# Inverting the delta rule's triangular blocks: 32-row blocks solved on VectorE, one level of TensorE products fewer

## What is computed

```python
m = jnp.einsum('bhncd,bhnsd->bhncs', k_beta, k) * decay
m = jnp.where(tri_strict, m, 0.0) + jnp.eye(CHUNK, dtype=jnp.float32)
rhs = jnp.concatenate([v * beta[..., None], k_beta * jnp.exp(g)[..., None]], axis=-1)
sol = lax.linalg.triangular_solve(m, rhs, left_side=True, lower=True, unit_diagonal=True)
u, w = sol[..., :dv], sol[..., dv:]
```

## Time and profile before

| | |
|---|---|
| median of 3 runs | 2465.13 us (2462.39 to 2465.59) |
| profiled execution, its own time | 2461.05 us |
| its span | 2459.3 us |
| TensorE matmul, busy | 2289.7 us, 93% |
| VectorE, busy | 1374.0 us, 56% |
| ScalarE, busy | 918.7 us, 37% |
| granted TensorE clock, mean | 0.972 |
| DMA | 328.93 MB, mean 134 GB/s |

### The profile page before, as it was taken

The page is one execution under the profiler, slowest core; times in us unless marked ns, Lnnn a source line. Parts: engine busy times, 40 slices in busy tenths (PEclk is TensorE's granted clock), DMA queues, the critical chain, the costliest instruction groups (busy, mean ns, idle before and its releaser), DMA issues. The chain is left out here.

```text
span 2459.3 us, 38535 instructions
## 1 busy us (share of the span) xinstructions
PE 2289.7 (93%) x13868; PEld 1852.7 (75%) x13868; DVE 1374.0 (56%) x2331; ACT 918.7 (37%) x1689; POOL 143.1 (6%) x183
## 2 busy tenths in 40 slices
PE   5789999999999999999999979899999999999887
PEld 3167787777778787878788758787887878787886
DVE  0334655546464646565654555656566565656665
ACT  3432424242433424242522363443424243342533
POOL 0000000000001000000100300000000000000002
PEclk8989999999999999999999989999999999999998
DMA  8974534243343435343545534433424343343554
GB/s 314 352 222 120 159 90 137 83 127 116 110 137 111 141 90 162 90 136 91 183 122 153 171 92 119 118 106 95 137 73 126 86 119 107 94 122 89 162 164 127
DMA packets 488882, 328.93 MB, mean 134 GB/s; under 512 B 48754, under 2 KB 452374, under 8 KB 488294
## 3 DMA queue, kind: packets, MB, share of 16 engines
q1 hardware_dynamic: 393750, 219.64, 31.6%
q10 hardware_dynamic: 94992, 108.09, 13.5%
q0 software_dynamic: 64, 0.20, 0.0%
HBM read 304.73 MB, written 23.13 MB: 133 GB/s over the span
## 5 line engine op out<-in xcount | busy, mean ns | idle before, releaser
L1808 PE MATMUL ps<-h_hi,w_hi 128*128 128x512 f32 (+1 forms) x2080 | 825.3, 397 | 18.1 <-DVE w_lo L1113 10.8
L1810 PE MATMUL ps<-h_hi,w_lo 128*128 128x512 f32 (+1 forms) x2080 | 768.1, 369 | 0.0
L1809 PE MATMUL ps<-h_lo,w_hi 128*128 128x512 f32 (+1 forms) x2080 | 767.6, 369 | 0.0
L1113 DVE TENSOR_TENSOR w_lo<-w_raw,w_hi 128x1024 fp32r<-128x1024 f32 (+1 forms) x300 | 365.4, 1218 | 290.6 <-ACT w_hi L660 251.4
L1808 PEld LDWEIGHTS ps<-h_hi,w_hi 128*128 128x128 f32 x2080 | 400.2, 192 | 125.3 <-issue 51.4
L660 ACT CAST w_hi<-w_raw 128x1024 fp32r<-128x1024 f32 (+1 forms) x300 | 311.5, 1038 | 369.5 <-PE ps L1810 188.0
L1810 PEld LDWEIGHTS ps<-h_hi,w_lo 128*128 128x128 f32 x2080 | 397.5, 191 | 68.5
L1809 PEld LDWEIGHTS ps<-h_lo,w_hi 128*128 128x128 f32 x2080 | 400.3, 192 | 49.8
L2089 PE MATMUL ps<-h_hi,w_hi 128*128 128x512 f32 (+1 forms) x448 | 157.8, 352 | 7.7 <-DVE h_lo L1113 6.6
L1648 POOL TENSOR_SCALAR small<-small 128x4 f32<-128x4 f32 (+3 forms) x51 | 20.5, 402 | 2254.5 <-DVE small L1488 987.4
L2090 PE MATMUL ps<-h_lo,w_hi 128*128 128x512 f32 (+1 forms) x448 | 151.7, 339 | 0.0
(11 more groups left out here) (199 smaller groups left out, 2769.7 us busy)
## 6 DMA issues: line engine op xcount, KB each, us to landing
w_raw<-in_w_in SPq DMA_DIRECT2D x260, 512.0 KB, 4.0
ada_raw<-in_w_ada ACTq DMA_DIRECT2D x128, 512.0 KB, 4.7
w_raw<-in_w_out SPq DMA_DIRECT2D x36, 448.0 KB, 3.8
arena<-in_w_ada SPq DMA_DIRECT2D x27, 512.0 KB, 8.4
arena<-in_w_out SPq DMA_DIRECT2D x28, 448.0 KB, 4.4
w_raw<-in_w_ada SPq DMA_DIRECT2D x19, 512.0 KB, 8.4
ada_raw<-in_w_ada SPq DMA_DIRECT2D x18, 512.0 KB, 8.3
arena<-decay_rows ACTq DMA_DIRECT2D x16, 512.0 KB, 6.2
```

The costliest lines, as they stand in the source:

```text
L1113: return V.tensor_tensor(o, a, b, op)
L1808: mm(o, w_hi[:, s, k], h_hi[:, kt, t0:], start=kt == 0, stop=False)
L1809: before_last = mm(o, w_hi[:, s, k], h_lo[:, kt, t0:], start=False, stop=False)
L1810: last = mm(o, w_lo[:, s, k], h_hi[:, kt, t0:], start=False, stop=kt == KT - 1)
```

## The change

The blocks that VectorE solves are 32 wide, so the product level from 16 to 32 goes. A block lies on four partitions: partition 32 q + b works on block b, on every fourth row of it (rows 4 i + q), so 8 rows each. All four hold the whole block of m (the read L590 becomes a broadcast to 128 partitions, 4 KB each). Row s of the inverse is found column by column: in step k the columns right of k get column k times row k of m taken off. Step k has k // 4 + 1 rows and 31 - k columns, a product and a subtraction. There are 31 steps in ten items (PIECES). The block stores and loads on SyncE are 4 DMAs in place of 8 each, and the solved blocks are stored by 4 DMAs in place of one. In the one full level left, inv is only formed in the quadrant that the corner step reads, so four of the eight matmuls and one of two merges shrink to 64x64. The slot tables are new.

```diff
-LEVELS = (16, 32, 64)
+LEVELS = (32, 64)
 BLK = LEVELS[0]
 NB = P // BLK
+SHARE = 4
+ROWS = BLK // SHARE
...
+        c[:, C_SHARE + q] = i // 32 == q
...
-        blocks = prod[0:2 * NT * NB].rearrange("p x c d -> p (x c d)")
-        blk_m, blk_s = [blocks[:, n * BLK * BLK:(n + 1) * BLK * BLK] for n in range(2)]
-        blk_t = blocks[:, 2 * BLK * BLK:4 * BLK * BLK]
+        blk_m = prod.rearrange("p x c d -> p (x c d)")
+        blk_s, blk_t = [inv_m[:, 0].rearrange("p c d -> p (c d)")[:, n * ROWS * BLK:(n + 1) * ROWS * BLK] for n in range(2)]
...
+        s_rows = blk_s.rearrange("p (i n) -> p i n", n=BLK)
+        s_diagonal = bass.AP(tensor=blk_s.tensor, offset=blk_s.offset,
+                             ap=[list(blk_s.ap[0]), [SHARE + BLK, ROWS], [1, SHARE]])
+
+        def eliminate(eng, own, steps):
+
             for k in steps:
-                up = SUB - 1 - k
-                term = t[:, :, 0:up, up:]
-                own.done(eng.tensor_tensor(term, m[:, :, 0:up, up:up + 1].to_broadcast(term.shape),
-                                           s_[:, :, up:up + 1, up:].to_broadcast(term.shape), ALU.mult))
-                own.done(eng.tensor_tensor(s_[:, :, 0:up, up:], s_[:, :, 0:up, up:], term, ALU.subtract))
-
-        def corner_product(eng, own, out_, a, b):
-
-            terms = blk_t.rearrange("p (r n k) -> p r n k", r=SUB, n=SUB)
-            own.done(eng.tensor_tensor(terms, a.unsqueeze(2).to_broadcast(terms.shape),
-                                       b.rearrange("p k n -> p n k").unsqueeze(1).to_broadcast(terms.shape), ALU.mult))
-            own.done(eng.tensor_reduce(out_, terms, AX, ALU.add))
-
-        def join_halves(eng, own):
-
-            spare = corner(blk_m, 1, 0)
-            corner_product(eng, own, spare, corner(blk_m, 0, 1), corner(blk_s, 1, 1))
-            corner_product(eng, own, corner(blk_m, 0, 1), corner(blk_s, 0, 0), spare)
-            own.done(eng.tensor_scalar(corner(blk_s, 0, 1), corner(blk_m, 0, 1), -1.0, None, ALU.mult))
+                rows = k // SHARE + 1
+                rest = BLK - 1 - k
+                term = blk_t[:, 0:rows * rest].rearrange("p (i n) -> p i n", n=rest)
+                own.done(eng.tensor_tensor(term, s_rows[:, 0:rows, k:k + 1].to_broadcast(term.shape),
+                                           blk_m[:, k * BLK + k + 1:(k + 1) * BLK].unsqueeze(1).to_broadcast(term.shape),
+                                           ALU.mult))
+                own.done(eng.tensor_tensor(s_rows[:, 0:rows, k + 1:], s_rows[:, 0:rows, k + 1:], term, ALU.subtract))
...
-        SUBST, SOLVED, LEVEL0 = {0: 12, 1: 15}, {0: 21, 1: 24}, {0: 23, 1: 26}
-        CORNERS = {0: 31, 1: 34}
-        V_SLOT = {0: (35, 41, 47, 53), 1: (37, 43, 48, 54)}
-        O_SLOT = {0: 56, 1: 57}
-        SCORE, TURN_P, ATTEND = {0: (3, 11, 19, 27), 1: (4, 16)}, {0: 5, 1: 6}, {0: 7, 1: 8}
+        PIECES = 10
+        SUBST, SOLVED, LEVEL0 = {0: 14, 1: 15}, {0: 29, 1: 31}, {0: 31, 1: 33}
+        CORNERS = {0: 36, 1: 38}
+        V_SLOT = {0: (40, 45, 50, 55), 1: (42, 46, 50, 54)}
+        O_SLOT = {0: 57, 1: 57}
+        SCORE, TURN_P, ATTEND = {0: (3, 12, 21, 30), 1: (4, 25)}, {0: 6, 1: 6}, {0: 8, 1: 8}
         TABLE_PE, TABLE_ACT = {0: (2, 5, 8), 1: (9, 16, 20)}, {0: (3, 6, 8), 1: (10, 17, 20)}
         TABLE_DVE = {0: (2, 4, 6, 8), 1: (9, 14, 16, 18)}
-        TURN_OA = {0: 38, 1: 30}
-        ROTATE = {0: (41, 43), 1: (34, 42)}
-        ADA_SLOT, ADA_EARLY = {0: (8, 12, 16, 20, 46, 52), 1: (10, 16)}, {0: 4, 1: 2}
-        BLOCKS_OUT, BLOCKS_BACK = {0: 7, 1: 7}, {0: 9, 1: 10}
+        TURN_OA = {0: 42, 1: 38}
+        ROTATE = {0: (45, 47), 1: (41, 43)}
+        ADA_SLOT, ADA_EARLY = {0: (8, 12, 16, 20, 50, 54), 1: (10, 16)}, {0: 4, 1: 2}
+        BLOCKS_OUT, BLOCKS_BACK = {0: 7, 1: 7}, {0: 11, 1: 12}
...
-        OUT_BLOCKS = {0: (9, 13), 1: (10, 15)}
+        OUT_BLOCKS = {0: (9, 18), 1: (10, 19)}
...
-                    sp.dma_start(blk_m, m_dram).then_inc(blocks_in, 16)
+                    sp.dma_start(blk_m, m_dram.unsqueeze(0).to_broadcast([SHARE, 2 * NT * NB, BLK * BLK])).then_inc(blocks_in, 16)
 
                 def blocks_back(i):
 
                     sp.wait_ge(blocks_solved, nth(layer, i, -1))
-                    sp.dma_start(s_dram, blk_s).then_inc(solved_out, 16)
-                    sp.wait_ge(solved_out, nth(layer, i, -1, 16, 16))
+                    for q in range(SHARE):
+                        sp.dma_start(s_dram.rearrange("b (i q n) -> q b i n", q=SHARE, n=BLK)[q],
+                                     s_rows[32 * q:32 * q + 32]).then_inc(solved_out, 16)
+                    sp.wait_ge(solved_out, nth(layer, i, -1, 16 * SHARE, 16 * SHARE))
...
-                    def substitute_backward(n):
+                    def solve_blocks(n):
 
                         if n == 0:
                             vec.wait_ge(blocks_in, h(-1, 16, 16))
                             vec.wait_ge(blk_identity, h())
-                        if n < 3:
-                            substitute(V, own, range(SUB - 1)[3 * n:3 * n + 3])
-                        else:
-                            join_halves(V, own)
+                        eliminate(V, own, range(BLK - 1)[3 * n:3 * n + 3 if n < PIECES - 1 else BLK])
+                        if n == PIECES - 1:
                             vec.sem_inc(blocks_solved, 1)
...
-                        own.go(tt(inv[:, d], inv[:, d], quads(GX[d]), ALU.subtract))
+                        part = inv[QUAD[d], d, :, QUAD[d]]
+                        own.go(tt(part, part, quads(GX[d])[QUAD[d], :, QUAD[d]], ALU.subtract))
...
-                    G.memset(blk_s[:, 0::BLK + 1], 1.0).then_inc(blk_identity, 1)
+                    G.tensor_copy(s_diagonal, share.unsqueeze(1).to_broadcast([P, ROWS, SHARE])).then_inc(blk_identity, 1)
...
-                            mm(quads(GX[d])[:, cc], inv_T[:, d, cc], prod[:, d, cc], start=True, stop=True)
-                            last = mm(quads(GT[d])[:, cc], prod[:, d, cc], inv_T[:, d, cc], start=True, stop=True)
+                            mm(quads(GT[d])[:, cc], prod[:, d, cc], inv_T[:, d, cc], start=True, stop=True)
+                            last = mm(quads(GX[d])[QUAD[d], cc, QUAD[d]], inv_T[QUAD[d], d, cc, QUAD[d]],
+                                      prod[QUAD[d], d, cc, QUAD[d]], start=True, stop=True)
```

More of the change, by code:

```diff
@@ L74 @@
 C_SEL = C_SIN + N_CTX
-C_END = C_SEL + 2
+C_SHARE = C_SEL + 2
+C_END = C_SHARE + SHARE
 def shape_constants():
@@ L102, in shape_constants @@
         c[:, C_SEL + v] = i % 32 == v
-    m = np.zeros((P, len(LEVELS), 2, P), np.float32)
-    for n, b in enumerate(LEVELS):
+    for q in range(SHARE):
+        c[:, C_SHARE + q] = i // 32 == q
+    m = np.zeros((P, len(LEVELS) - 1, 2, P), np.float32)
+    for n, b in enumerate(LEVELS[:-1]):
         blk = i // b
@@ L182, in build_trunk @@
         cst = sb("cst", [P, C_END])
-        msk = sb("msk", [P, len(LEVELS), 2, P], BF16)
+        msk = sb("msk", [P, len(LEVELS) - 1, 2, P], BF16)
         vecs = sb("vecs", [P, 4, P])
@@ L274, in build_trunk @@
         sel = cst[:, C_SEL:C_SEL + 2]
+        share = cst[:, C_SHARE:C_SHARE + SHARE]
         TAB_BETA, TAB_GROW, TAB_END, TAB_G, TAB_LAST = range(5)
[L277 to L287, removed]
@@ L289, in substitute @@
-        def substitute(eng, own, steps):
-            m, s_ = diagonal_halves(blk_m), diagonal_halves(blk_s)
-            t = blk_t[:, 0:2 * SUB * SUB].rearrange("p (h r n) -> p h r n", h=2, r=SUB)
-            for k in steps:
-                up = SUB - 1 - k
-                term = t[:, :, 0:up, up:]
-                own.done(eng.tensor_tensor(term, m[:, :, 0:up, up:up + 1].to_broadcast(term.shape),
-                                           s_[:, :, up:up + 1, up:].to_broadcast(term.shape), ALU.mult))
-                own.done(eng.tensor_tensor(s_[:, :, 0:up, up:], s_[:, :, 0:up, up:], term, ALU.subtract))
@@ L1539, in body @@
                             put(s + TURN_P[layer] - (3 if layer and n == 0 else 2), a_mix, n)
-                        for n in range(4):
-                            put(SUBST[layer] + n, substitute_backward, n)
+                        for n in range(PIECES):
+                            put(SUBST[layer] + n, solve_blocks, n)
                         put(SOLVED[layer], turn_inv, 0)
```

## The result

The changed kernel takes 2571.11 us (median of 4 runs, 2567.94 to 2575.97), the kernel before 2463.76 (4 runs, 2454.96 to 2465.59): a ratio of 1.0446, 95% interval 1.0426 to 1.0466. That is 107 us slower, 106 above the forecast and 61 above the range. The profiled execution took 2567.94 us.

The account below looks back on a forecast made before the run. TensorE was taken as the bound, with VectorE mattering where its queue is late. -87.4 + 11 - 73.8 + 73.5 + 8 + 28.7 + 34 + 5.6 = -0.4 us gave 2464.7 us; range 2415 to 2510.

Parts of the forecast that it names:

- the fetch of the m blocks: Before the solve: 512 KB instead of 64; layer 1 issue at 1663.8, solve from 1669.6; layer 0 blocks at 688.3, before 687.50.
- until a weight load is late: Condition on counting the added DMA bytes, 7 MB of 329, at nothing, hidden by DMA engines 0.4 busy.
- the small matmuls: Remaining product level: 64x64 matmuls alternating with full ones add 0.09 us a pair, +11 us, bounds -21 and +26.
- the clock: Half clock after new waits: 2.5 us a head in layer 1, 2.0 in layer 0, +34; old stretches removed, -21.9.
- products -87.4: TensorE: one of two full product levels goes in both directions, 5.46 us a head, 87.4 us over 16 heads.
- The old waits: TensorE's waits inside the heads, 51.9 us, go with their steps; with seven half-clock stretches, -73.8 us.
- The solve: VectorE: 62 operations for the 31 steps take 15.1 us a head in ten pieces, sharing slots with splits and taps.
- The wait at turn_p in layer 1: TensorE in slot 31 waits for the mixed scores about 10.5 us in 7 heads, 73.5; last head 8.
- the forecast of 4.1 us a head: Layer 0, turn in slot 27: TensorE at 711.1 waits for the mix until 715.4, in 7 heads 28.7 us.
- The way back: Storing and reloading solved blocks on SyncE: 3.9 us each leg, blocks turned in layer 1 just when TensorE reaches times_m.
- the 6.8 of the rival: Rival on the way back: each store takes 6.8 us, so TensorE waits at times_m; +38, 2503 us; chance 0.23.
- the gain on TensorE is given back as waits: Whole sum: TensorE's saving is offset by new waits, -0.4 us, median 2464.7; forecast case's chance 0.50.

Follow-up runs that it names:

- g1_half_solve: e2_grouped with the last 16 of the solve's 31 steps left out, so the inverse is incomplete; 2401.3 us, ratio 0.975 to the kernel before.
- e2_grouped: The changed kernel with the fetch as four reads and, in times_inv, four full matmuls first, then four 64x64; 2468.5 us, ratio 1.003 to the kernel before.
- e1: The changed kernel with the broadcast fetch of the m blocks issued as four reads of 128 KB; 2503.8 us, ratio 1.016 to the kernel before.
- b1: The kernel before plus one unused 256 KB broadcast load a head behind the fetch, awaited before the solve; 2558.8 us, ratio 1.038.
- b2: The kernel before plus the same unused 256 KB as in b1, but as four DMAs of 16 rows; 2496.3 us, ratio 1.014.

## Why the prediction was wrong

**The step that failed** is the fetch of the m blocks: "It now moves 512 KB, not 64. Such a load lands in 4.0", with "costs at nothing: the added DMA bytes (7 MB of 329), hidden by DMA engines that are 0.4 busy". Rows 9 are of loads that keep 12 packets in work at once, not four. Of the broadcast the trace of before had no row, and the nearest one was no bound from above. The sum had 5.8 us from the fetch's issue to the solve in layer 1, and in layer 0 a start 0.8 us later than before. It took 14.8 us in a head of layer 1 and 11.1 in one of layer 0 (682.43 to 693.49), where the kernel before has 2.2. The larger loss had no term at all: the wait of TensorE for ada weights, 110.4 us where it was 14.9. The prediction named the condition, "until a weight load is late", and put no price on it. The run with four reads puts 67 us of the 107 on the form of the fetch. The Trainium skill, DMA: Bandwidth & Descriptors, says in its Rules for kernel authors that a leading zero-stride broadcast of c copies confines the whole DMA to at most c engines. The trace agrees, by the window at 0.26 and by 3.2 to 3.8 packets at once, and the prediction did not use it. It was also wrong to average the DMA share over a head: the 0.39 of this head of layer 1 is 0.80 over the 15 us that count.

**The second failed term is the small matmuls.** I put +0.10 for each turn and half of 0.225 for the small one, +11 us in all with an upper bound of +26. Measured are +0.93 a call, 32 × 0.93 = +30, and 31 to 35 us in the runs. The nearest row, a full projection matmul before one of 32 rows, gave 0.10; in the midst of a call a full matmul and a 64x64 one take 0.22 more than two full ones.

**The third is the clock.** The sum had +34 for new stretches at the lower level and -21.9 for old ones, +12 together. In the clock records of the two traces the lower level is granted for 306 us of the span, 140 before, and TensorE is busy for 177 us of it, 103 before. At half speed that is an estimate of +37 us.

With these the account nearly closes, by the waits of the two traces: products -87.4 + 30, ada wait +95.5, turn_p +56.5 (12.9 to 69.4), the other old waits -32.6, clock +37, together +99 of the 105.7 us between the two spans.

**Right were:**
- The old waits went: those of L1736, L1908 and L1897 were 39.0 us and are 6.4.
- The solve. In layer 1 it runs from 1819.65 to 1841.3, splits and taps inside, in layer 0 from 693.49 to 718.1: 21.7 and 24.6 us. The terms gave 21.7 and 24.9 for the same items. Only its start, 8 to 10 us after the first store by the forecast, was wrong: 18.6 and 16.4.
- The wait at turn_p in layer 1: 7.9 to 9.4 a head, 10.5 forecast. That the size fits is partly luck, since both sides came late: VectorE by the fetch, TensorE by the ada load. g1_half_solve shows that the wait hangs on the solve's length. In layer 0 the forecast of 4.1 us a head, at the turn of slot 27, was wrong: no wait is there in the changed kernel or in e2_grouped (the 0.8 us a head at L1978 is the turn of the first score). The mix began at 720.0 and not at 714.3, but TensorE came at 720.56 and not at 711.1. 4.6 us of this are waits at the ada product. The rest is mostly TensorE's own way there, which the sum had too short: from the turn of slot 14 to that of slot 27 e2_grouped takes 28.5 us, 3.3 of them idle, against 23.0.
- The way back, by a small margin. The store takes 3.9 us in layer 0 (718.21 to 722.13), as assumed, and 4.5 in layer 1 (1844.14 to 1848.64), far from the 6.8 of the rival but over the 3.9 from which the prediction had it decide there. times_m never waits: in this head the blocks are turned at 1852.65 and it starts at 1853.82. The rival that ended slower would have given a slower kernel for a reason that was not there.
- That the gain on TensorE is given back as waits. e2_grouped, with both errors of the edit repaired, stands at 2468.5 us against a forecast of 2464.7. That is partly luck: turn_p waits 78 us there and not 110, the ada product 57 where I had added nothing to the 15 of before.

What stays open: e1's share of 67 us is measured as a whole. Its trace puts the gain on the loads that were held up, not on turn_p: the ada wait falls by 54 us, and the wait at turn_p rises from 69.4 to 74.9, since TensorE now comes there earlier too. What the earlier solve is worth by itself in this kernel was not taken apart; in b1, where the ada loads are not held up, a late solve alone costs 64 us against b2.

## What to carry to other kernels

A DMA is not priced by its bytes alone: look at how many of its packets are in work at once, and write a broadcast of four copies as four DMAs, one for each (3.2 to 3.8 packets at once against 4.6 to 13.3 here). Before placing a transfer that something waits for, list what is issued within its landing time on every queue, and take the DMA share of that stretch, not of the loop. When the queue of one engine bounds a stage, moving the steps behind it changes only where the wait shows; first make its input earlier.

## What had not been expected of the hardware

- A broadcast fetch with four packets at once slows other loads: an ada half of 512 KB issued 0.5 us behind it took 14.9 us to land in the head shown, 7.6 to 8.7 when the same bytes came as four reads, and 4.6 on the median of the program.
- A full and a 64x64 float32 matmul in turn take 0.67 us a pair, against 0.45 for two full ones. In a group behind four full ones, four of them take 0.73 us (1.71 less 0.98) and are cheaper than four full ones, 0.90.
- Moving a pair of 512 KB loads by six slots in each head of layer 1, with no change in work, was worth 34 us of 2468.
